# A search among 112 pair sums, and the per-layer gate and the final norm in one stage

## The reference, cut to what matters

```python
# experts: for each token and each of 8 heads
v1, i1 = lax.top_k(s1, 16);  v2, i2 = lax.top_k(s2, 16)          # two lists, sorted
cand = (v1[..., :, None] + v2[..., None, :]).reshape(..., 256)
sc, ci = lax.top_k(cand, 16)
e = i1[ci // 16] * 128 + i2[ci % 16];  g = softmax(sc)
x = x + sum_k (g * gelu(x_normed . u[e])) * v[e]
# per-layer input and final norm
x = x + sigmoid(rmsnorm(x, g_ple) @ w_ple_gate) * (p @ w_ple_proj)
y = rmsnorm(x, g_final)                                           # x / sqrt(mean(x^2) + eps) * g
```

## Time and profile before

| | us |
|---|---|
| runs | 2289.80, 2292.68, 2292.78 |
| median | 2292.68 |
| profiled execution: its own time | 2291.48 |
| its span, first to last instruction | 2289.9 |
| busy in the span: PE | 2116.7 (92%) |
| DVE | 1357.3 (59%) |
| POOL | 556.4 (24%) |
| ACT | 359.7 (16%) |

### The profile page before, as it was taken

The page is one execution under the profiler, slowest core; times in us unless marked ns, Lnnn a source line. Parts: engine busy times, 40 slices in busy tenths (PEclk is TensorE's granted clock), DMA queues, the critical chain, the costliest instruction groups (busy, mean ns, idle before and its releaser), DMA issues. The chain is left out here.

```text
span 2289.9 us, 24728 instructions
## 1 busy us (share of the span) xinstructions
PE 2116.7 (92%) x8879; PEld 1581.6 (69%) x8879; DVE 1357.3 (59%) x2821; ACT 359.7 (16%) x743; POOL 556.4 (24%) x516
## 2 busy tenths in 40 slices
PE   6958999966999998899999999999699999999997
PEld 4746677743889966677767777777477777777776
DVE  2005377762444259599999999988635446436232
ACT  1001146650010111211111222222000000000011
POOL 1001000022000000232235555454534344334000
PEclk9988999987559999999999999999899999999998
DMA  3142221123022332488789999999999999999320
GB/s 128 47 71 67 68 101 47 37 59 112 34 113 89 118 110 92 159 284 286 262 292 348 405 401 395 398 404 407 400 379 348 361 387 382 379 364 351 113 101 38
DMA packets 166865, 511.69 MB, mean 223 GB/s; under 512 B 18286, under 2 KB 52726, under 8 KB 163159
## 3 DMA queue, kind: packets, MB, share of 16 engines
q1 hardware_dynamic: 93782, 273.61, 33.4%
q0 software_dynamic: 60288, 213.96, 24.6%
q10 hardware_dynamic: 12672, 22.55, 2.6%
HBM read 460.32 MB, written 49.72 MB: 223 GB/s over the span
## 5 line engine op out<-in xcount | busy, mean ns | idle before, releaser
L1863 PE MATMUL ex_ps<-h,ex_ring 128*128 128x320 f32 x2048 | 570.5, 436 | 9.7 <-DMA ex_ring<-in_uT 5.9
L1918 PE MATMUL ex_ps<-proj,ex_ring 128*128 128x320 f32 x2048 | 557.3, 435 | 20.8 <-DMA ex_ring<-in_v 20.8
L1918 PEld LDWEIGHTS ex_ps<-proj,ex_ring 128*128 128x128 f32 x2048 | 391.9, 192 | 185.9 <-DMA ex_ring<-in_v 22.0
L1863 PEld LDWEIGHTS ex_ps<-h,ex_ring 128*128 128x128 f32 x2048 | 386.6, 192 | 162.5 <-issue 8.4
L2094 DVE TENSOR_TENSOR proj<-proj 128x320 f32<-128x320 f32 x124 | 53.0, 489 | 253.5 <-DMA proj<-scratch_a 233.7
L2028 DVE SCALAR_TENSOR_TENSOR gx_sum<-proj,gx_sum 128x1024 f32<-128x1024 f32 x120 | 154.1, 1284 | 8.8 <-DVE gx_sum L2028 0.5
L2010 DVE CUSTOM_DVE_ANT_0 proj<-proj,gx_tokens 128x1024 f32<-128x1024 f32 x120 | 143.8, 1221 | 1.6 <-DMA proj<-in_u,at_last 1.2
L1765 POOL DMA_INDIRECT scores<-in_u,at_last x26 | 31.8, 1222 | 451.8 <-POOLq L1496 407.7
L1771 POOL DMA_INDIRECT proj<-in_v,at_last x76 | 105.8, 1392 | 85.6 <-DVE gx_sum L2028 69.7
L1765 POOL DMA_INDIRECT proj<-in_u,at_last x76 | 88.1, 1159 | 148.5 <-DVE proj L2010 136.0
L379 PE MATMUL gate_ps<-h,work 128*128 128x260 f32 x512 | 120.4, 389 | 3.1 <-DMA work<-in_w_t 3.1
(11 more groups left out here) (372 smaller groups left out, 2795.4 us busy)
## 6 DMA issues: line engine op xcount, KB each, us to landing
ex_ring<-in_uT SPq DMA_DIRECT2D x128, 512.0 KB, 6.7
ex_ring<-in_v SPq DMA_DIRECT2D x128, 512.0 KB, 6.6
scratch_a<-ex_gelu ACTq DMA_DIRECT2D x64, 320.0 KB, 7.2
scratch_w<-proj SPq DMA_DIRECT2D x10, 2048.0 KB, 11.5
proj<-scratch_a SPq DMA_DIRECT2D x15, 1280.0 KB, 9.9
proj<-scratch_w SPq DMA_DIRECT2D x15, 1280.0 KB, 10.9
work<-in_w_t SPq DMA_DIRECT2D x37, 512.0 KB, 3.6
mg_ring<-in_w_q SPq DMA_DIRECT2D x32, 512.0 KB, 3.5
```

The source lines that it names most:

```text
L1863: last = nc.tensor.matmul(y[:, bank(n), 0:TD], u[:, n % UR, k, :], xn[:, k, 0:TD], start=(k == 0), stop=(k == DC - 1))
L1918: last = nc.tensor.matmul(y[:, m, 0:TD], ring[:, (E1 + e) % UR, m * P:(m + 1) * P], hidden_of(part_of[e])[:, e - parts[part_of[e]][0], :], ...
```

## The change

Three edits.

1. In `select_slots` the sums of a head are made for 112 pairs and not 256: the first 4 of list one with all 16 of list two, and the other 12 with the first 4 of list two. (A pair at places a and b, both 4 or more, has at least 24 other pairs that are no smaller.) The winner's place in this list of 112 is turned back into a and b by four integer operations, one conversion and four more operations.
2. In `experts`, `EXP_AT` and `DOTS_AT` name earlier tiles.
3. `per_layer_input` and `final_norm` become one stage, `finish`. The gate's matmuls run on `x * g_ple`, not yet divided by the root, and the product is multiplied by the inverse root afterwards (`rt`). The sum of squares goes over the chunks on VectorE first, then over the partitions by 5 matmuls with one column, so that root and reciprocal work on 5 columns; 5 matmuls with the identity spread the result back over the partitions. The squares of the final norm are taken and summed tile by tile.

```diff
-    link(nc.vector.tensor_tensor(cd[0:m, 0:nh], vv[:, :, 0, :].unsqueeze(3).to_broadcast([m, nh, PK, PK]),
-                                 vv[:, :, 1, :].unsqueeze(2).to_broadcast([m, nh, PK, PK]), ALU.add))
+    for (a0, a1), nb, at in (((0, FEW), PK, 0), ((FEW, PK), FEW, FEW * PK)):
+        na = a1 - a0
+        done = nc.vector.tensor_tensor(
+            cd[0:m, 0:nh, at:at + na * nb].rearrange("p h (a b) -> p h a b", a=na),
...
+    link(done)
...
-    nc.vector.tensor_scalar(cb[0:m, 0, 0:nh], ci[0:m, 0:nh], 4, None, ALU.logical_shift_right)
-    link(nc.vector.tensor_scalar(cb[0:m, 1, 0:nh], ci[0:m, 0:nh], PK - 1, None, ALU.bitwise_and))
-    nc.vector.tensor_copy(cf[0:m, :, 0:nh], cb[0:m, :, 0:nh])
+    for j, (k, op) in enumerate(((4, ALU.logical_shift_right), (2, ALU.logical_shift_right),
+                                 (PK - 1, ALU.bitwise_and), (FEW - 1, ALU.bitwise_and))):
+        done = nc.vector.tensor_scalar(cb[0:m, j, 0:nh], ci[0:m, 0:nh], k, None, op)
+    link(done)
+    link(nc.vector.tensor_copy(bf[0:m, :, 0:nh], cb[0:m, :, 0:nh]))
+    by16, by4, in16, in4 = (bf[0:m, j, 0:nh] for j in range(4))
+    nc.vector.scalar_tensor_tensor(out=cf[0:m, 0, 0:nh], in0=by4, scalar=float(FEW - PK), in1=by16, op0=ALU.add, op1=ALU.max)
+    link(nc.vector.tensor_tensor(in4, in4, in16, ALU.subtract))
+    link(nc.vector.scalar_tensor_tensor(out=in4, in0=by16, scalar=float(FEW), in1=in4, op0=ALU.is_ge, op1=ALU.mult))
+    nc.vector.tensor_tensor(cf[0:m, 1, 0:nh], in16, in4, ALU.add)
...
-    EXP_AT = {tile_at(us): i for i, us in enumerate((74, 157, 202))}
-    DOTS_AT = [min(W0 - 1, tile_at(18 + 15.2 * k)) for k in range(PRE_CHUNKS + 1)]
+    EXP_AT = {tile_at(us): i for i, us in enumerate((70, 148, 190))}
+    DOTS_AT = [min(W0 - 1, tile_at(18 + 14.2 * k)) for k in range(PRE_CHUNKS + 1)]
...
+def finish(nc, I, c, x, h, dst):
...
+        @block.sync
+            for n in range(DC):
+                if n >= RING:
+                    sp.wait_ge(s_pb, n - RING + 1)
+                sp.dma_start(ring[:, n % RING], I["w_gp"][n]).then_inc(c.slots.sems[n % RING], 16)
+                if n == 0:
+                    sp.dma_start(pT[:, :, :], I["pT"]).then_inc(s_i, 16)
...
+            def logits(n):
+                pe.wait_ge(*c.slots.landed(n))
+                if n >= 2:
+                    pe.wait_ge(s_lg, n - 1)
...
+            def inputs(n):
+                pe.wait_ge(s_i, 16)
+                if n >= 1:
+                    pe.wait_ge(s_gd, n)
...
+            logits(0)
+            first.sums(pe)
+            logits(1)
+            first.spread(pe, flat_b)
+            pe.wait_ge(s_rt, 1)
+            inputs(0)
+            for n in range(2, DC):
+                logits(n)
+                inputs(n - 1)
+            inputs(DC - 1)
+            final.sums(pe)
+            final.spread(pe, flat_a)
...
+        @block.scalar
+            for k in range(DC):
+                nc.scalar.activation(sq[:, k, :], x[:, k, :], ACT.Square).then_inc(s_sq, 1)
+            first.roots(act)
+            act.wait_ge(first.s_spread, 1)
+            nc.scalar.copy(rt[:, :], flat_b[:, 0:N]).then_inc(s_rt, 1)
+            for n in range(DC):
+                act.wait_ge(s_lg, n + 1)
+                nc.scalar.activation(lg[:, n % 2, :], lg[:, n % 2, :], ACT.Sigmoid).then_inc(s_sg, 1)
+                if n == DC - 1:
+                    nc.scalar.activation(idle[:, :], c.eps[:, 0:1], ACT.Sqrt)
+                act.wait_ge(s_x, n + 1)
...
+                nc.scalar.activation(sq[:, n, :], x[:, n, :], ACT.Square).then_inc(s_fq, 1)
+            final.roots(act)
...
+            for n in range(DC):
+                dve.wait_ge(s_pa, n + 1)
...
+                nc.vector.tensor_tensor(halves(lg[:, n % 2, :]), pa[:, n % 2, :, 0:HALF], halves(rt[:, :]),
+                                        ALU.mult).then_inc(s_lg, 1)
+                gate(n)
+                if n >= 2:
+                    sum_up(n - 1)
+            sum_up(DC - 1)
```

More of the change, by code:

```diff
@@ L1450, in merge_tail @@
     return a.sems
+FEW = 4
+CAND = FEW * PK + (PK - FEW) * FEW
 class Picker:
@@ L2106, in experts, with __init__, sums, roots @@
         nc.release_semaphore(sem)
-def per_layer_input(nc, I, c, xn, x):
+class Root:
+    def __init__(self, nc, c, sq, total, root, inv, sem, ps_sum):
+        self.nc, self.c, self.sq, self.total, self.root, self.inv = nc, c, sq, total, root, inv
+        self.ps_sum = ps_sum
+        self.s_total, self.s_sum, self.s_root, self.s_inv, self.s_spread = (
+            sem(k) for k in ("squares_added", "sums", "roots", "inverted", "spread"))
+        self.starts = [t * P for t in range(NT)] + [N - P]
+    def sums(self, pe):
+        pe.wait_ge(self.s_total, 1)
+        for t, n0 in enumerate(self.starts):
+            last = self.nc.tensor.matmul(self.ps_sum[:, t:t + 1], self.total[:, n0:n0 + P], self.c.ones[:, 0:1],
+                                         start=True, stop=True)
+        last.then_inc(self.s_sum, 1)
+    def roots(self, act):
+        act.wait_ge(self.s_sum, 1)
+        self.nc.scalar.activation(self.root, self.ps_sum, ACT.Sqrt, scale=1.0 / D,
+                                  bias=self.c.eps[:, 0:1]).then_inc(self.s_root, 1)
+    def invert(self, dve):
+        dve.wait_ge(self.s_root, 1)
+        self.nc.vector.reciprocal(self.inv, self.root).then_inc(self.s_inv, 1)
+    def spread(self, pe, out):
+        pe.wait_ge(self.s_inv, 1)
+        for t in range(NT):
+            self.nc.tensor.matmul(out[:, t * P:(t + 1) * P], self.inv[:, t:t + 1].to_broadcast([P, P]), self.c.ident[:, :],
+                                  start=True, stop=True)
+        self.nc.tensor.matmul(out[:, TP:N], self.inv[:, NT:NT + 1].to_broadcast([P, P]), self.c.ident[:, P - TS:P],
+                              start=True, stop=True).then_inc(self.s_spread, 1)
+def finish(nc, I, c, x, h, dst):
     RING = 4
@@ L2133, in _ @@
+            sp.wait_ge(s_o, 16 * DC // 2)
         @block.tensor
         def _(pe):
-            norm.sums(pe)
-            pe.wait_ge(s_i, 16)
-            for n in range(DC):
+            def logits(n):
                 pe.wait_ge(*c.slots.landed(n))
                 if n >= 2:
[L2140 to L2149, removed]
+                    pe.wait_ge(s_lg, n - 1)
+                for k in range(DC):
+                    if n == 0:
+                        pe.wait_ge(s_xg, k + 1)
+                    for j in range(2):
+                        last = nc.tensor.matmul(pa[:, n % 2, j, 0:HALF], ring[:, n % RING, k, :],
+                                                h[:, k, j * HALF:(j + 1) * HALF], start=(k == 0), stop=(k == DC - 1))
+                last.then_inc(s_pa, 1)
@@ new lines, in inputs @@
+            def inputs(n):
+                pe.wait_ge(s_i, 16)
+                if n >= 1:
+                    pe.wait_ge(s_gd, n)
+                for k in range(PC):
+                    for j in range(2):
+                        last = nc.tensor.matmul(pb[:, j, 0:HALF], ring[:, n % RING, DC + k, :],
+                                                pT[:, k, j * HALF:(j + 1) * HALF], start=(k == 0), stop=(k == PC - 1))
+                last.then_inc(s_pb, 1)
+            logits(0)
+            first.sums(pe)
@@ L2151, in _ @@
+            logits(1)
[8 more added lines that the diff above has]
+            final.spread(pe, flat_a)
         @block.scalar
         def _(act):
-            norm.squares(act)
-            for n in range(DC):
[L2155 to L2158, removed]
+            for k in range(DC):
+                nc.scalar.activation(sq[:, k, :], x[:, k, :], ACT.Square).then_inc(s_sq, 1)
@@ L2160, in _ @@
+            final.roots(act)
         @block.vector
         def _(dve):
-            norm.scale(dve)
-            for n in range(DC):
-                dve.wait_ge(s_s, n + 1)
+            for k in range(DC):
+                nc.vector.tensor_scalar(h[:, k, :], x[:, k, :], c.small["g_ple"][:, k:k + 1], None,
+                                        ALU.mult).then_inc(s_xg, 1)
+            dve.wait_ge(s_sq, DC)
+            for i, m in enumerate((DC // 2, DC // 4, DC // 8)):
+                if i:
+                    dve.wait_ge(s_tree, i)
+                nc.vector.tensor_tensor(sq[:, 0:m, :], sq[:, 0:m, :], sq[:, m:2 * m, :], ALU.add).then_inc(
+                    s_tree if m > 1 else first.s_total, 1)
@@ L2170, in _, with sum_up @@
                 nc.vector.tensor_tensor(x[:, n, :], x[:, n, :], gd[:, n % 2, :], ALU.add).then_inc(s_x, 1)
-            dve.wait_ge(s_x, DC)
[L2174 to L2200, removed]
+            def sum_up(n):
+                dve.wait_ge(s_fq, n + 1)
+                if n >= 2:
+                    dve.wait_ge(s_sum, n - 1)
+                nc.vector.tensor_tensor(sq[:, 0, :], sq[:, 0, :], sq[:, n, :], ALU.add).then_inc(
+                    s_sum if n < DC - 1 else final.s_total, 1)
@@ L2203 @@
+            dve.wait_ge(s_x, DC)
+            for k in range(DC):
```

(3 more changed lines are left out.)

59 lines of the change are left out of this document (42 added, 17 removed).

## The result

The changed kernel takes 2266.3 us, median of 4 runs (2264.91 to 2267.32); the kernel before took 2292.73 in the same job (2289.8 to 2293.24, 4 runs). The ratio is 0.9889, 95% interval 0.9873 to 0.9904: 26.4 us faster, where 28.5 was forecast. The profiled execution of after took 2267.32 us, with a span of 2265.7.

What follows compares the result with a forecast made beforehand. TensorE was taken to bound the kernel, except for waits in the head, experts and last stages. Gains 3.3 + 11.7 + 13.5 = 28.5 us from 2291.48 gave 2263.0 us, own range 2259 to 2269, wider range 2256 to 2275.

Steps and rivals of the forecast that it cites:

- Head: Head stage: cheaper sums and three searches let VectorE start the reciprocal earlier, shortening TensorE's wait; 3.3 us.
- Experts: Experts stage: TensorE's waits for a gelu and one-hot rows end, with the slow time after; 5.3, 3.75 and 2.65, 11.7 us.
- the third exponential: Experts stage: ScalarE's wait for VectorE, with all gelus behind it; ready 14.4 us earlier, at 1168.6.
- the positions alone are worth nothing: Experts stage: earlier places in EXP_AT and DOTS_AT gain nothing alone, since ACT waits at them for VectorE.
- One stage: The merged last stages: earlier first products and a shorter chain at the end; 13.5 us, bounds 7 and 18.
- The behaviour at the end: Last stage: behind the last tile, a chain through VectorE, sums, spread, scalings and last store, together 20.0 us.
- the first load: Start of the last stage: tile 0's weights, first in the queue, land in 3.8 us; bound 3.6 to 4.9.
- starts badly: Rival, last stage: weights late and TensorE idle between the first two tiles, 6 us lost, 2269; chance 0.13.
- beyond 11.7 there is nothing: After the experts' gain of 11.7 us: no further change, because TensorE is full from there in both kernels.
- The price of a wait: TensorE is slow after idling: a wait of about 3 us costs its length and another 1.6 to 2.9 us.
- slower: Rival, last stage's steady part: a long gating chain idles TensorE in every tile; 35 us with an 11 us chain, 2298; 0.02.
- The table load: Last stage: root's table load and empty root, 1.5 us, lie beside gating and addition; by the skill, last square 1.1 later.

Runs made afterwards that it cites:

- the early load: The changed kernel with the gate's first weight tile loaded at the end of the experts' own DMA queue, into memory free by then: 2259.84 us.
- the search alone: The changed kernel (search among 112 sums, new positions) with the two old stages at the end put back: 2274.15 us.
- the finish alone: The kernel before with the new last stage, keeping the search among 256 and the old positions: 2280.78 us.
- the chain got shorter: The changed kernel with factor and sigmoid of tile n + 1 ahead of tile n's gating, and another bank for tile 7's input products: 2263.29 us.
- everything together: The changed kernel with early weights, first sums behind tile 1's products, 7 filling products, shorter chain, and the head's scaling one search earlier: 2253.47 us.

## Why the prediction was right, and where its sizes were off

**Head: 3.3 forecast, 3.27 found** (from the last output tile's products to the query products: 865.91 - 819.06 = 46.85 us, before 866.98 - 816.86 = 50.12). A search cost 1.63 us, and its five instructions 0.26 to 0.28 us each, so the price by the length held down to 112 places.

**Experts: 11.7 forecast, 12.08 found** (from the first product to the second gate weights: 1200.65 - 952.21 = 248.44 us, before 1213.77 - 953.25 = 260.52). Counted from that first product, the third exponential came 14.5 us earlier; 14.4 was forecast. The splitting, counted as before from the subtraction on (1024.04 to 1026.72), takes 2.7 us, as forecast; before, it was five instructions in 1.1 us and not six. That the positions alone are worth nothing held in both directions; the reason I gave for it was that ScalarE waits for VectorE there, and the old search with the new positions shows just that.

**One stage: 13.5 forecast, 12.47 found.** The behaviour at the end was right almost to the step: from the gating of tile 6 (2245.71) to the end of the span it is 19.99 us, forecast as 20.0. In it the additions took 0.4 less, slow sums and slow spread with handovers 0.7 more, the scalings 0.2 less. The mis-sized term is the first load: products began 4.7 us after its issue, not 3.8. I took the fastest landing of the earlier trace rows; this first one took longer than the median there, 4.4, within the bound of 4.9 that I had given. The rest of the rival "starts badly", TensorE idle between the first tiles, did not come: 0.68 us is the only wait there. How much lies in that place the early load showed: 5.1 us by the trace, weights and slow products together, in an execution where the products were not slow. And 12.47 is the gain over one execution of the old stages. In the kernel with the search alone the same old stages took 3.1 us less, and against that execution the new stage gains 9.4 (114.3 against 104.9); the finish alone gained 11.1 by its median. So the forecast of 13.5 is rather too high, by 1 to 4 us: it took the slow products of before's execution for what these stages always have.

**A term I did not have: 1.4 us given back in the v half.** From the first product with v to the end of them, before took 2172.53 - 1597.00 = 575.53 us and after 2160.82 - 1583.91 = 576.91. I had written that beyond 11.7 there is nothing because TensorE is full from there; it is not, where u ends and v begins. There it waits three times for a load of v: 2.42, 11.07 and 7.32 us in before, 2.45, 12.80 and 7.26 in after. No load is late by itself: from the first product with v to the end of the second wait it is 30.18 us in before, 30.29 in after, and 30.15 to 30.31 in all ten profiled kernels, and the third wait is 7.19 to 7.43 us in all ten, however long the work ahead of it took. What got longer is the work behind the second and third wait. The 40 products behind the second, in before and in after, with the columns of the earlier trace rows:

```profile
1627.18:1650.87 23.69, 23.69 (x80) 16.18 (x80) 23.16 (x38) 0.61 (x3) 18.81 (x16) 0.92 1.03 403
1614.20:1638.75 24.55, 24.55 (x80) 16.70 (x80) 23.99 (x41) 0.77 (x4) 19.12 (x16) 0.89 1.03 403
```

They took 0.86 us more at a lower mean clock (length times clock is 21.8 us in both), and the last group from 1658.19 and 1646.02 on another 0.46, with 0.82 and 0.78 granted in its first 10 us. From the start of one group to that of the next, the second is 30.70 to 31.01 us long in the three profiled kernels with the old search (clock 0.92 to 0.93) and 31.29 to 31.98 in all seven with the new one (0.88 to 0.91). Why the clock stays low for longer there is open.

So the account is 3.27 + 12.08 + 12.47 - 1.38 = 26.4, the difference of the medians. That the two agree to 0.1 us is luck, as the runs of one kernel lie 2 to 3 us apart; the forecast differs from it by 0.4 in the experts, 1.0 in the one stage (0.9 of it the first load) and 1.4 in the v half.

**The price of a wait.** I put 1.6 to 2.9 us of slow products behind a wait of some 3 us, and in the rival "slower" I let it begin at some 2.5 us of idling. In the experts that held: with the finish alone both waits were followed by the slow rows of before. But it is no fixed price, and 2.5 us is no border: behind 1.47 us the first 16 products of the old last stages took 8.97 us in before; the first 32 products with v took 19.12 us behind 2.42 in before and 17.49 behind 2.45 in after; the last sums took 2.30 and 1.34 us behind the same 3.4.

**The table load.** It began 0.01 us after the last sigmoid (2248.40 + 0.64 and 2249.05) and took 1.28 us; root and load were done at 2250.54, and the addition beside them at 2250.50. The Trainium skill, ScalarE: Activation LUTs, section What ACT_TABLE_LOAD costs, gives about 2.66 us for a switch, the load and a drain together. No drain shows here, neither ahead of the load nor behind it, so the trace decides against that figure. By the trace the load was hidden with nothing to spare: once the chain got shorter, it delayed the last square by 0.14 us.

## What to carry to other kernels

When an engine off the path works through a long queue, price what it is late for: some 14 us of VectorE's work was worth 12 us to TensorE, as two waits and the slow products behind each of them ended on it, and moving the other engine's places in the order was worth nothing. Where waits for transfers stand behind the place of a gain, compare how long the work behind each of them takes before calling the gain whole. A load that opens a stage belongs into the queue of the stage before it; here that took 5.1 us out of the trace. And 8 products that nobody reads, put into 3.4 us of idling, made the small matmuls behind it cheaper, by 2.3 us in the trace.

## What was not expected

- After the same wait, the opening products of the last stage ran either at full speed or slowly. With the early weights alone they took 7.25 us after 1.43 of idling, with everything together 8.94 after 1.43; the sums of squares of the old stage took 7.28 after 1.45 in the kernel with the search alone, and 8.97 after 1.47 in before:

```profile
2165.11 7.28 PE L143 MATMUL pl_ps_a<-pl_sq,ones 128*128 128x260 f32 x32 [1.45 <-ACT pl_sq L132]
```

  The granted clock goes with it. Early in the opening products it was 0.50 with everything together (first row) and 1.00 with the early weights alone (second row):

```profile
2167.00:2169.00 2.00, 2.00 (x6) 1.57 (x5) 1.13 (x3) 2.00 (x5) 0.00 (x0) 0.50 1.01 378
2168.00:2170.00 2.00, 2.00 (x11) 1.74 (x10) 0.96 (x4) 1.98 (x5) 0.00 (x0) 1.00 0.99 404
```

  So 1.7 us behind a short wait come or stay away; one execution of each does not tell on what that depends.
- Ahead of the head stage, where all ten profiled kernels have the same code up to the picks, the query products began anywhere from 859.66 us (with the filling) to 868.34 (old search, new positions). The head's wait explains 3.4 us of that (8.53 against 5.15); the rest is from execution to execution, and more than some of the terms discussed. Stretches between two rows tell more than two spans do.
